# Down products in quarters between the next expert's gate and up products, and weights fetched in the order of their use

## What is computed

```python
def expert_block(args):
    xb, e = args
    return (jax.nn.silu(xb @ w1[e]) * (xb @ w3[e])) @ w2[e]
```

## Time and profile before

| | us |
|---|---|
| median of 3 runs (1719.05 to 1720.77) | 1719.24 |
| time of the profiled execution | 1718.73 |
| its span in the trace | 1716.9 |
| PE busy in the span | 1602.3 (93%) |
| DVE busy | 673.9 (39%) |
| ACT busy | 403.1 (23%) |
| mean granted TensorE clock, of full speed | 0.982 |

### The profile page before, as it was taken

How to read it: one execution, slowest core, us unless ns; L and a number is a source line. 1 busy time by engine, 2 the same in 40 slices (tenths; PEclk the granted TensorE clock), 3 DMA queues, 4 the chain that set the end, 5 groups by cost and what they waited for, 6 DMA issues and landing times. The chain is left out here.

```text
span 1716.9 us, 37104 instructions
## 1 busy us (share of the span) xinstructions
PE 1602.3 (93%) x15957; PEld 1039.2 (61%) x15957; DVE 673.9 (39%) x1682; ACT 403.1 (23%) x897; POOL 176.2 (10%) x220
## 2 busy tenths in 40 slices
PE   5999999998999999999999999999999999999873
PEld 3444445896777787644444445556777776676652
DVE  3533324312767667766654456562101001000003
ACT  4100000002666667510010002212121211211112
POOL 1205000000111010000000000001111111111100
PEclk8999999998999999999999999999999999999997
DMA  9874232235111007434352162289999999999996
GB/s 345 263 222 108 84 98 99 76 102 173 35 44 45 33 3 241 122 104 132 115 155 86 38 245 111 86 341 366 356 391 395 386 382 399 392 391 404 410 406 259
DMA packets 163745, 362.38 MB, mean 211 GB/s; under 512 B 28631, under 2 KB 111183, under 8 KB 138971
## 3 DMA queue, kind: packets, MB, share of 16 engines
q1 hardware_dynamic: 141456, 316.12, 50.1%
q0 software_dynamic: 12608, 28.01, 6.2%
q10 hardware_dynamic: 9516, 15.85, 2.6%
HBM read 323.48 MB, written 48.50 MB: 217 GB/s over the span
## 5 line engine op out<-in xcount | busy, mean ns | idle before, releaser
L2779 DVE TENSOR_TENSOR sb_m_hT<-psum,sb_m_sg 128x256 f32<-128x256 f32 (+2 forms) x32 | 15.3, 477 | 299.7 <-PE psum L2895 299.7
L2616 ACT ACTIVATE sb_w_o_sb<-psum,sb_rowmod 128x64 f32<-128x64 f32 (+2 forms) x256 | 81.7, 424 | 206.4 <-PE psum L2883 206.4
L862 PE MATMUL psum<-sb_vD,sb_room 128*128 128x512 f32 x240 | 104.7, 592 | 0.2 <-DVE sb_vD L743 0.2
L2895 PE MATMUL psum<-sb_w_o_sb,sb_front 128*64 128x64 f32 (+2 forms) x2560 | 91.0, 231 | 11.9 <-issue 7.3
L2895 PEld LDWEIGHTS psum<-sb_w_o_sb,sb_front 128*64 128x64 f32 x2560 | 89.0, 138 | 18.8 <-issue 18.2
L1179 ACT ACTIVATE sb_d_probs<-sb_d_probs,sb_d_nmax 128x640 f32<-128x640 f32 (+7 forms) x128 | 92.9, 735 | 12.6 <-DVE sb_d_nmax L1220 12.1
L1777 PE MATMUL psum<-sb_w_o_sb,sb_room 128*128 128x512 f32 x192 | 85.7, 603 | 0.0
L862 PEld LDWEIGHTS psum<-sb_vD,sb_room 128*128 128x128 f32 x240 | 45.5, 190 | 57.9 <-issue 57.9
L1148 PE MATMUL psum<-sb_vS,sb_room 128*64 128x65 f32 x2112 | 80.0, 226 | 0.3 <-ACT sb_room L1166 0.3
L1133 PE MATMUL psum<-sb_const,sb_d_probs 128*128 128x128 f32 x528 | 77.3, 283 | 1.6 <-ACT sb_front L1179 0.7
L1166 ACT COPY sb_room<-psum 128x512 f32<-128x512 f32 (+1 forms) x108 | 59.3, 549 | 82.6 <-PE psum L1133 82.6
(11 more groups left out here) (466 smaller groups left out, 2702.1 us busy)
## 6 DMA issues: line engine op xcount, KB each, us to landing
sb_front<-in_exp_w_dram SPq DMA_DIRECT2D x30, 2048.0 KB, 24.0
sb_mT<-in_exp_w_dram SPq DMA_DIRECT2D x20, 2048.0 KB, 26.6
sb_room<-in_exp_w_dram SPq DMA_DIRECT2D x18, 2048.0 KB, 23.9
sb_rows<-in_exp_w_dram SPq DMA_DIRECT2D x18, 2048.0 KB, 23.3
sb_w_o_sb<-in_exp_w_dram SPq DMA_DIRECT2D x10, 2048.0 KB, 25.1
sb_g_ada<-in_ada_w_dram SPq DMA_DIRECT2D x16, 1024.0 KB, 5.2
d_qk<-sb_n_b_sel ACTq DMA_DIRECT2D x20, 512.0 KB, 3.4
sb_front<-in_w_in_dram SPq DMA_DIRECT2D x16, 512.0 KB, 5.3
```

What stands on the lines that cost most here:

```text
L862: mm = pe.matmul(k.psum[:, bank(g, i), :], w[:, kk, :], x[:, kk, :], start=(kk == 0), stop=(kk == KD // 2 - 1))
L2616: last = act.activation(dst[:, kk, 0:w], src, ACT.Identity, scale=k.rowmod[:, 0, kk:kk + 1], bias=k.rowmod[:, 1, kk:kk + 1])
L2779: tt(hT[:, :, 0:width[b]], hidden_ps(1, width[b]), sg[:, :, 0:width[b]], ALU.mult).then_inc(s_hid, 1)
L2895: mm = pe.matmul(k.psum[part, which, c * w:(c + 1) * w], view[:, kk, first:first + 2 * CAPS - 1:2], x[:, kk, 0:w], start=(kk == 0), stop=( ...
```

## The change

The change has three parts. The down products of a block no longer stand in its own turn of the loop: for blocks 0 to 29 they stand in four parts in the next block's turn, one behind each half of the gate products and one behind each half of the up products. Blocks 30 and 31 have their down products whole, as before. `turn` of the next block stays behind the up products, which is now the end of a block's turn. DVE makes `hidden` of block `b + 1` ahead of the weighted output of block `b`. And the weights are fetched in the order in which the products now come: gate of `b`, down of `b - 1`, up of `b`. With that, `stage_out` fetches loads 0 to 4 and 6, since load 5 is now the gate matrix of block 2, whose expert isn't known there; two slots of the ring change places for it.

```diff
+def load_order():
+    loads = [(0, 0), (0, 1)]
+    for b in range(1, NE - 1):
+        loads += [(b, 0), (b - 1, 2), (b, 1)]
+    return loads + [(NE - 2, 2), (NE - 1, 0), (NE - 1, 1), (NE - 1, 2)]
...
-AHEAD, FETCHED = 3, 6
+AHEAD, FETCHED = 3, (0, 1, 2, 3, 4, 6)
...
+            for n, (b, i) in enumerate(loaded):
+                if n in FETCHED:
+                    continue
+                if i == 0:
+                    expert[b] = sp.value_load(be_i[0:1, order[b]:order[b] + 1], min_val=0, max_val=NE - 1)
...
+                if n >= RING:
+                    last, part = loaded[n - RING]
+                    sp.wait_ge((s_gate, s_up, s_y)[part], last + 1)
...
             for b in range(NE):
-                if b >= 1:
-                    hidden(b)
+                if 1 <= b + 1 < LAST:
+                    hidden(b + 1)
+                elif b == LAST:
+                    hidden(LAST)
                 dve.wait_ge(s_y, b + 1)
...
+            def ready(b):
+                if b >= 2:
+                    pe.wait_ge(s_ys, b - 1)
+                if b == 0:
+                    pe.wait_ge(s_idx, 2)
+                if b == 1:
+                    pe.wait_ge(s_be, 1)
+                landed(b, 2)
+                pe.wait_ge(s_hid, b + 1)
+
+            def downs(b, some):
+                for c in some:
+                    mm = down(c, width[b], 4 + 2 * (b % 2), down_w(slot_of(b, 2)))
+                if KE - 1 in some:
+                    mm.then_inc(s_y, 1)
...
+                if mixed:
+                    project(0, width[b], xT[b % 2], gate_w(slot_of(b, 0)), some=halves[0])
+                    ready(b - 1)
+                    downs(b - 1, (0,))
+                    project(0, width[b], xT[b % 2], gate_w(slot_of(b, 0)), some=halves[1]).then_inc(s_gate, 1)
+                    downs(b - 1, (1,))
                 else:
...
+                if mixed:
+                    project(1, width[b], xT[b % 2], gate_w(slot_of(b, 1)), some=halves[0])
+                    downs(b - 1, (2,))
+                    project(1, width[b], xT[b % 2], gate_w(slot_of(b, 1)), some=halves[1]).then_inc(s_up, 1)
+                    downs(b - 1, (3,))
                 else:
...
                 if 1 <= b and b + 1 < NE:
                     pe.wait_ge(s_g[(b + 1) % 2], gathers(b + 1))
                     turn(xg[(b + 1) % 2], width[b + 1], s_turned)
...
-                for c in range(KE):
-                    mm = down(c, width[b], 4 + 2 * (b % 2), down_w(slot_of(b, 2)))
-                mm.then_inc(s_y, 1)
+                if b >= LAST - 1:
+                    ready(b)
+                    downs(b, range(KE))
```

More of the change, by code:

```diff
@@ L2461, in stage_moe @@
         width = [capacity(r) for r in order]
-        slot_of = lambda b, i: (3 * b + i) % RING
-        loads = lambda b, i: 16 * ((3 * b + i) // RING + (0 if (3 * b + i) % RING < FETCHED else 1))
+        loaded = load_order()
+        place = {load: n for n, load in enumerate(loaded)}
+        slot_of = lambda b, i: place[b, i] % RING
+        loads = lambda b, i: 16 * (place[b, i] // RING + (0 if place[b, i] % RING in FETCHED else 1))
         LAST = NE - 1
-        free = [slot_of(LAST - 2, 0), slot_of(LAST - 2, 1), slot_of(LAST - 2, 2), slot_of(LAST - 3, 2)]
+        free = [slot_of(LAST - 2, 0), slot_of(LAST - 2, 1), slot_of(LAST - 1, 0), slot_of(LAST - 3, 2)]
         ya = [ring[free[t // 4]][:, (t % 4) * D:(t % 4 + 1) * D] for t in range(NT)]
@@ L2485, in _ @@
         def _(sp):
[L2486 to L2499, removed]
+            expert = {}
+            for n, (b, i) in enumerate(loaded):
[3 more added lines that the diff above has]
+                    expert[b] = sp.value_load(be_i[0:1, order[b]:order[b] + 1], min_val=0, max_val=NE - 1)
+                if n == SPARE:
+                    sp.wait_ge(s_onehots, 2)
+                    sp.wait_ge(s_slots, 1)
+                if n >= RING:
+                    last, part = loaded[n - RING]
+                    sp.wait_ge((s_gate, s_up, s_y)[part], last + 1)
+                w = (k.exp_w1, k.exp_w3, k.exp_w2)[i]
+                sp.dma_start(*expert_matrix(w, bass.ds(expert[b], 1), ring[slot_of(b, i)], i == 2)).then_inc(s_w[slot_of(b, i)], 16)
             sp.wait_ge(s_y, LAST - 1)
@@ L2885, in turn, with project @@
                 tr.then_inc(done, 1)
-            def project(which, w, x, view, rest=None):
-                for c in range(KE):
+            def project(which, w, x, view, rest=None, some=range(KE)):
+                for c in some:
                     for kk in range(KD):
@@ L2906, in landed @@
             def landed(b, i):
-                if b < KNOWN:
-                    pe.wait_ge(k.s_first[3 * b + i], 16)
+                if place[b, i] in FETCHED:
+                    pe.wait_ge(k.s_first[FETCHED.index(place[b, i])], 16)
                 else:
@@ L2917, in _ @@
+            halves = (range(KE // 2), range(KE // 2, KE))
             for b in range(NE):
+                mixed = 1 <= b < LAST
                 pe.wait_ge(s_xT, b + 2 if b else 1)
-                if b == 0:
-                    pe.wait_ge(k.s_first[0], 16)
-                else:
[L2922 to L2926, removed]
-                else:
-                    pe.wait_ge(s_hid, b)
-                    landed(b, 1)
@@ L2930, in _ @@
-                project(1, width[b], xT[b % 2], gate_w(slot_of(b, 1))).then_inc(s_up, 1)
+                if b >= 1:
+                    pe.wait_ge(s_silu, b)
+                landed(b, 0)
+                if mixed:
[4 more added lines that the diff above has]
+                    downs(b - 1, (1,))
+                else:
+                    project(0, width[b], xT[b % 2], gate_w(slot_of(b, 0)), 0 if b else 2).then_inc(s_gate, 1)
@@ new lines, in _ @@
+                if b >= 1:
+                    pe.wait_ge(s_hid, b)
+                landed(b, 1)
+                if mixed:
[3 more added lines that the diff above has]
+                    downs(b - 1, (3,))
+                else:
+                    project(1, width[b], xT[b % 2], gate_w(slot_of(b, 1))).then_inc(s_up, 1)
@@ L2978, in build @@
         k.s_dil4 = k.sem("dilated_set4_stored")
-        k.s_first = [k.sem(f"first_expert{i}") for i in range(FETCHED)]
+        k.s_first = [k.sem(f"first_expert{i}") for i in range(len(FETCHED))]
         k.s_kT, k.s_brow_out, k.s_tables = k.sem("cmp_rows"), k.sem("bias_rows"), k.sem("bias_tables")
```

23 lines of the change are left out of this document (6 added, 17 removed).

## The result

The changed kernel takes 1802.8 us as the median of five runs (1798.85 to 1806.93) against 1719.24 before: 1.0487 times as long, with a 95% interval of 1.0471 to 1.0504. 1807 was forecast. The profiled execution has a span of 1805.1 us (before 1716.9) and a mean granted clock of 0.958 (before 0.982).

What follows compares the result with a forecast made beforehand. PE was taken to set the pace for 24 of 32 blocks, the weights' stream the end. Last down product: 1672.3 + 84.8 - 1.5 + 6 + 18 = 1779.6 against 1692.0; so 1718.73 + 87.6 + 1 = 1807 us, range 1782 to 1836.

Steps and rivals of the forecast that it cites:

- The stall, 84.8 us: Behind `turn` for blocks 1 to 30, PE stands still while ACT works, 2.74 to 3.06 us each: 84.8 us.
- The clock, 18 us from 12 falls: Behind the 30 new idle times, two in five restarts at the lower clock, 1.5 us each: 18 us, bounds 0 to 45.
- each stall costs the clock: Rival: all 30 restarts behind the stalls run at the lower clock, 27 us more, 1834 us; chance 0.10.
- The "issue" waits: PE's waits of no shown cause, 20.9 us in 18 before, were kept at 1.16 us in a narrow block.
- 90 changes between down and `project`, 6 us: On PE, down products change place with `project` three times more a block: 6 us, bounds nothing to 14.
- `hidden`, -1.5 us: PE's down products no longer wait for DVE's `hidden` in wide and middle blocks: -1.5 us.
- The slack, 19.7 us: PE could be 19.7 us slower over the stage before the end moves, since the weights' stream sets the end.
- The end, +1: Behind the last down product, adding block 30's rows has less time to finish: 1 us, bounds nothing to 3.
- The order of loads, nothing: The new order of weight loads and later return of down matrices cost nothing, hidden because PE gets slower.
- without that cover 1 to 3 us, in the first blocks: Were PE not slower, the new order of loads would cost 1 to 3 us in the first blocks.

Runs made afterwards that it cites:

- experiment 1: Changed kernel with `turn` of the next block moved between the two halves of the up products: 1732.48 us, 1.0072 times the kernel before.
- experiment 4: Changed kernel with useless products added on PE in the wait for ACT, blocks 1 to 29: four gave 1779.87 us, three 1763.35 us.
- experiment 3: Kernel before with `turn` moved behind the whole down products for blocks 1 to 29, nothing mixed, old load order: 1822.6 us, 1.0588 times before.
- experiment 6: Changed kernel with `turn` between the up halves, and blocks 0 to 13 as before, mixing and new load order only from block 14: 1724.11 us.
- experiment 5: Changed kernel with `turn` between the up halves and the old load order: 1737.14 us; conversely, the kernel before with the new load order alone: 1721.28 us.
- experiment 2: Changed kernel with `turn` moved ahead of the last down part, so only that part covers ACT: 1734.23 us, 1.0092 times before.

## Why the prediction was right, and which of its sizes were not

The mechanism and the direction were right: PE stands still behind each `turn` for as long as ACT works. By the terms of the sum:

- **The stall, 84.8 us.** Measured 79.4 us of idle time in 30 waits, 2.56 for narrow blocks and up to 2.9 for wide ones. The mechanism is right, and experiment 1 shows it. The term was 5.4 us too large: it had added 0.27 us to ACT's run at each stall, and the rows have 0.03 ahead of it (1701.18 to 1701.21) and 0.06 behind (1703.68 to 1703.74).
- **The clock, 18 us from 12 falls.** Mis-sized. There were 25 falls, and experiment 4 puts them at 39 us (36 more than the kernel before, whose two falls would be 3 at the same rate, an estimate). The price of a fall was right (1.5 forecast, 1.6 measured); the count was not. I had counted two falls in five idle times of over 2 us in the trace of before and carried the share over. The five were not all: among those left out is one of 4.85 us up to 394.21, with a granted clock of 0.50 from 394 to 398. There such idle times stood apart; here one comes in every block. Whether that is why a larger share of them costs the clock, no run tells. The rival "each stall costs the clock" was nearer: 25 of 30. The rule that I had weighed against the trace, of the Trainium skill, "TensorE: Matmul & The Clock Gate", section "HAM oscillation — how this bites in real kernels", agrees with this trace in 25 restarts of 30, better than my share from the rows did, and in 18 of the 29 of experiment 3. The match is a loose one, since the kernel of that page waits 3 to 5 us for transfers before each tile, and PE here 2.56 to 2.88 for ACT. The five that escaped came behind 2.56 and 2.67 us, as most of the others did, and why they did is open.
- **The "issue" waits.** The prediction let them stand at 1.16 us in a narrow block. That step failed: 27.7 us in the stage became 3.3, a gain of 24.4 that no term held. Experiment 3 shows that the stall alone does not bring it, and every kernel that mixes down parts into all the projections has only 3 to 8 us of them, once the waits for down matrices of experiment 1 are taken out. What these waits are, the views of waits don't say, but the record of transfers does. The page has a queue that loads instructions, in packets of 16 KB (before, whole span):

```profile
q8 instruction: 129, 2.11, 0.5%
```

The stage before has 70 of these packets for PE's 17,900 matmuls and weight loads, one for each 256. If the waits ahead of down parts are left aside (in experiments 1 and 6), 129 "issue" waits of over 0.4 us stand in the stages of the twelve kernels, and each of them ends 1.2 to 1.7 us after such a packet; of moments taken at random in a stage, 6 to 7% do. So PE waits for its instructions. In the mixed kernels such waits come back in the last two blocks, whose down products are whole (1693.13 and 1699.17 in experiment 1). Why down parts between the projections take the waits away is only argued: a down product, 3.65 / 16 = 0.23 us a record against 4.06 / 128 = 0.03 for one of `project`, gives the loading of instructions time to keep up.
- **90 changes between down and `project`, 6 us.** About right. The parts follow each other without idle time, but those of wide and middle blocks take longer than in one piece. Down of the wide block 10, after the change:

```profile
1407.75 1.97 PE L2914 MATMUL psum<-sb_mT,sb_m_hT 128*112 128x512 f32 x4
1409.65 2.14 PE L2907 MATMUL psum<-sb_w_o_sb,sb_front 128*64 128x64 f32 x64
1411.72 1.97 PE L2914 MATMUL psum<-sb_mT,sb_m_hT 128*112 128x512 f32 x4
1413.62 2.14 PE L2907 MATMUL psum<-sb_w_o_sb 128*64 128x64 f32 x64
1415.69 1.97 PE L2914 MATMUL psum<-sb_mT,sb_m_hT 128*112 128x512 f32 x4
1417.59 2.14 PE L2907 MATMUL psum<-sb_w_o_sb 128*64 128x64 f32 x64
1419.66 1.97 PE L2914 MATMUL psum<-sb_mT,sb_m_hT 128*112 128x512 f32 x4
1421.47 1.12 PE L2895 MATMUL psum<-sb_const,sb_g1row 128*128 128x128 f32 x8
```

and the row behind the down products that start at 1352.80 before the change:

```profile
1359.82 4.07 PE L2895 MATMUL psum<-sb_w_o_sb,sb_mT 128*64 128x64 f32 x128
```

From the start of a part to the start of what follows it is 1.90, 1.90, 1.90 and 1.81, that is 7.51 us, against 1359.82 - 1352.80 = 7.02 in one piece. The seven middle blocks (7.40 against 7.00) show 0.4 each, the narrow ones 3.53 against 3.48. That makes some 6 us in the 13 wide and middle blocks. What in the changes of place takes this time, no run tells.
- **`hidden`, -1.5 us.** Waits for it are 0.7 us in the stage against 1.8 before, so -1.1: right.
- **The slack, 19.7 us.** No landing ends a wait of PE, and the median load lands 12.6 us after its issue from 1500 to 1780, where it was 36.7: the stream of weights no longer sets the end, as forecast.
- **The end, +1.** The tail was 24.4 us against 24.9: no cost.
- **The order of loads, nothing.** Right for the changed kernel, and experiment 5 finds nothing for it alone. But "without that cover 1 to 3 us, in the first blocks" was mis-sized: place right, size not. The later return of slots, not the order, costs some 9 us of stage in experiment 1 (537.2 against 528.4), and one slot fewer costs the kernel before 7.6.

Two errors hid each other. The clock cost 21 us more than its term, and the vanished "issue" waits gave back 24.4. The stage's account is then 79.4 (stall) + 36.3 (clock) - 24.4 ("issue") - 1.1 (`hidden`) - 14.1 (landing waits) = 76.1, against the 83.4 measured. The 7.3 us left are of the size of the turns above, and experiments point the same way: if all waits are taken from a stage, and 39.1 / 95.6 = 0.41 us for each us at the lower level (an estimate), PE's work is 482 us before, 483 to 486 in the four other kernels with whole down products (experiment 3, with its 29 stalls, has 483), and 488 to 489 in the four with all of them in parts and no added products. So it goes with the parts and not with the stalls. That the forecast came within 0.3% is luck in part: two terms were wrong by over 20 us each, in opposite directions.

What the 12 us of experiment 1 are made of is shown for the greater part: a gap in the transfers in blocks 1 and 2 that goes with the mixing and leaves with it, that nine slots alone bring about, and behind which every later load is 9 to 10 us late (load 13 by 9.5, the last by 9.3). That it is all of the 12 us is not shown, since experiment 6 left 3.6 of them.

## What to carry to other kernels

When work is moved into finer pieces, look first at what the moved piece was covering: here the down products stood between the transposes and the products that need them, and 2.5 us of ACT's work came out into the open thirty times. An idle time of PE that recurs in every block has two prices, its length and the slower restart behind it; putting useless products that fit into it shows the second by itself. A wait that the profile calls "issue" can be one for a transfer, of weights or of instructions: compare its end with the landings and with the packets of the instruction queue before leaving it unexplained. Take the stall away before judging the rest of a change, since it covers smaller costs (here slots that come back late) that decide the result once it is gone.

## What the runs showed of the hardware

- Idle times of PE of 2.56 to 2.9 us in each block let the clock fall in 25 cases of 30, at 1.6 us each, and in 18 of 29 in experiment 3; 29 waits of 0.84 to 1.55 us let it never fall (experiment 2).
- "Issue" waits of PE in the middle of its products end 1.2 to 1.7 us after a 16 KB packet of the instruction queue, 129 times of 129. Those of some 1.2 us a block went almost wholly away when the 256 short products of a block were broken up by down parts of 512 columns (27.7 to 3.3 us).
- A product with 512 columns in float32 is two records, and a further one in a row of them takes 3.60 - 2.74 = 0.86 us (experiment 4), where I had taken 0.55.
- Ten slots in flight fill the DMA engines (share 1.00 between 1185 and 1205 us), nine leave them at 0.73 and cost 7.6 us; the new load order alone leaves them at 0.80 and costs nothing that could be measured.
- Down products of 112 rows take 7.02 us as 16 records in a row and 7.51 in four parts between other products.
